# Second-layer projections as one phase of seven block products, with rows through memory and turned in each attention

## The reference, cut to what matters

```python
def dilated_mixer(h, w_in, q_norm, k_norm, positions):
    q, k, v, xq = split_cols(h @ w_in, [nh * DIL_HEAD_DIM] * 3 + [D_XA])      # nh = 12
    q = apply_rope(rms_norm(hs(q), q_norm), cos, sin)
    k = apply_rope(rms_norm(hs(k), k_norm), cos, sin)
    for g, (window, dilation) in enumerate(DIL_GROUPS):                        # (128, 1), (512, 4), (2048, 16)
        sl = slice(g * DIL_HEADS, (g + 1) * DIL_HEADS)
        o, lse = dilated_window_attention(q[:, :, sl], k[:, :, sl], v[:, :, sl], window, dilation)
    wts = jax.nn.softmax(jnp.stack(lses), axis=0)
    o = jnp.sum(wts[..., None] * jnp.stack(outs), axis=0)
```

## Time and profile before

| | us |
|---|---|
| median of three runs | 2442.65 (2440.76 to 2444.62) |
| the profiled execution | 2440.05 |
| its span in the profile | 2438.3 |
| TensorE matmul busy | 2383.5 (98%) |
| VectorE busy | 1709.8 (70%) |
| ScalarE busy | 1020.6 (42%) |
| GpSimd busy | 201.3 (8%) |

### The profile page before, as it was taken

One profiled execution on the slowest core, in us unless ns is written; L12 is line 12 of the kernel. 1 busy time (PEld: TensorE's weight loads), 2 busy tenths in 40 slices (PEclk: granted clock), 3 DMA queues, 4 the chain that ended last, 5 costly groups with the idle time before them and its releaser, 6 DMA issues. The chain is left out here.

```text
span 2438.3 us, 31873 instructions
## 1 busy us (share of the span) xinstructions
PE 2383.5 (98%) x11700; PEld 2021.3 (83%) x11700; DVE 1709.8 (70%) x2782; ACT 1020.6 (42%) x2078; POOL 201.3 (8%) x269
## 2 busy tenths in 40 slices
PE   8999999999999999999999999999999999999998
PEld 7998877888888888878788889888888888888877
DVE  4432574489999989896553462463779999998996
ACT  6433553344444444436334442333344444444443
POOL 2010021000000000002212121112100000000000
PEclk9999999999999999999999999999999999999999
DMA  4331122222222248843102111202722222227863
GB/s 154 92 92 22 37 85 67 81 80 78 84 90 87 78 136 303 272 131 139 53 18 83 36 35 48 63 30 75 219 89 83 82 78 85 88 87 258 293 190 127
DMA packets 207666, 257.69 MB, mean 106 GB/s; under 512 B 38504, under 2 KB 141912, under 8 KB 207512
## 3 DMA queue, kind: packets, MB, share of 16 engines
q1 hardware_dynamic: 203352, 255.65, 31.9%
q10 hardware_dynamic: 4160, 0.02, 0.1%
HBM read 206.54 MB, written 49.09 MB: 105 GB/s over the span
## 5 line engine op out<-in xcount | busy, mean ns | idle before, releaser
L52 PE MATMUL psum<-f_T_lo 128*128 128x512 f32 x616 | 241.6, 392 | 1.4 <-DVE f_T_lo L690 0.8
L53 PE MATMUL psum<-f_T_lo 128*128 128x512 f32 x616 | 239.8, 389 | 0.0
L54 PE MATMUL psum<-f_T_lo 128*128 128x512 f32 x616 | 239.8, 389 | 0.0
L52 PE MATMUL psum<-w_hi,hT_hi 128*128 128x512 f32 x576 | 229.3, 398 | 4.2 <-DVE w_lo L1476 2.1
L54 PE MATMUL psum<-w_hi,hT_lo 128*128 128x512 f32 x576 | 226.4, 393 | 0.0
L53 PE MATMUL psum<-w_lo,hT_hi 128*128 128x512 f32 x576 | 226.1, 393 | 0.0
L52 PEld LDWEIGHTS psum<-w_hi,hT_hi 128*128 128x128 f32 x576 | 124.8, 217 | 22.3 <-issue 3.9
L52 PEld LDWEIGHTS psum<-f_T_lo 128*128 128x128 f32 x616 | 115.6, 188 | 30.5 <-DVE f_T_lo L690 7.1
L54 PEld LDWEIGHTS psum<-w_hi,hT_lo 128*128 128x128 f32 x576 | 125.0, 217 | 18.0
L53 PEld LDWEIGHTS psum<-w_lo,hT_hi 128*128 128x128 f32 x576 | 125.1, 217 | 16.6
L52 PE MATMUL psum<-hT_hi,f_up_hi 128*128 128x512 f32 x352 | 137.4, 390 | 0.4 <-DVE f_up_lo L629 0.4
(11 more groups left out here) (432 smaller groups left out, 5919.2 us busy)
## 6 DMA issues: line engine op xcount, KB each, us to landing
raw<-in_ffn_w_up_dram SPq DMA_DIRECT2D x88, 512.0 KB, 4.7
activations<-f_act SPq DMA_DIRECT2D x44, 512.0 KB, 2.6
w_raw<-in_b_w_in_dram SPq DMA_DIRECT2D x18, 1024.0 KB, 5.7
f_up_pieces<-activations SPq DMA_DIRECT2D x30, 512.0 KB, 4.4
f_up_pieces<-in_ffn_w_down_dram SPq DMA_DIRECT2D x22, 512.0 KB, 4.8
x_between<-XY SPq DMA_DIRECT2D x16, 512.0 KB, 5.0
XY<-x_between SPq DMA_DIRECT2D x16, 512.0 KB, 6.8
w_raw<-in_a_w_in_dram SPq DMA_DIRECT2D x8, 768.0 KB, 5.6
```

The costliest lines, as they stand in the source:

```text
L52: nc.tensor.matmul(out, lhs_hi, rhs_hi, start=start, stop=False)
L53: nc.tensor.matmul(out, lhs_hi, rhs_lo, start=False, stop=False)
L54: return nc.tensor.matmul(out, lhs_lo, rhs_hi, start=False, stop=stop)
```

## The change

All projections of the second layer are done in one new phase, `rows_phase`, before the three attentions.

- The four remaining tiles of cross queries are computed first. Then six chunks follow, two for each group. A chunk has four column blocks of 384: two halves of q (or of k) of 256 columns, each beside 128 columns of v; they form a 2 x 2 block scheme with the two halves of the tokens and the two halves of the inner dimension. Each chunk is seven products of (512 tokens x 512) by (512 x 384). A product is 4 tiles x 4 parts x 3 matmuls of 384 columns.
- The token sums S1, S2, S4 are made on VectorE (high parts on ScalarE), S3 wholly on GpSimd, once. The weight differences T1 to T4 are made on VectorE for each chunk.
- The products are combined on VectorE (`put`), partly into kept tiles, partly into 16 row tiles of 128 x 384 per chunk. Row tiles stand in a ring of seven slots (`RING`). For each row tile ScalarE squares and sums two heads, GpSimd takes the root and multiplies the crossed halves by the sine, VectorE multiplies by the cosine (`turn`), GpSimd adds, ScalarE scales by the root, and SP stores the tile to memory. The gains are multiplied into the tables of sine and cosine beforehand, on GpSimd. Which tiles are squared in which product is a table, and they are scaled one product later.
- The attentions load the rows again, token tiles in the group's order, 128 x 1536 each (four blocks, each with two heads of queries or keys and one head of values). `Turns` turns queries and keys of one tile after the other in the midst of the attention's steps, in one PSUM bank: queries copied by ScalarE, keys by VectorE. In the first attention the cross queries are turned in steps 8 to 11.
- SP issues row loads at the start of the first attention (tiles 4 to 7 of its own group, the cross rows, all eight tiles of the next group), then the keys and values, then the output stores. The third group's rows are loaded during the second attention.
- `SlotsAhead` and the tile `zeros` go, and the turns in `Merge` move from steps 5 and 14 to 14 and 16.

```diff
+B11, B12, B21, B22 = range(4)
+R11, SUM2, SUM4, SUM3, R22, R12, R21 = range(7)
+BLOCK, ROPED = 384, 256
+RING = 7
+SQUARED_IN = {2: (0, 1), 3: (2, 3), 5: (4, 5, 6), 6: (7, 8, 9), 7: (10, 11, 12), 8: (13, 14, 15)}
+SCALED_IN = {p + 1: quads for p, quads in SQUARED_IN.items()}
+def rows_phase(nc, ph, psum, neg_half, hT_hi, hT_lo, ...):
...
+        W11, W21, T2, T1, T3, W22, T4 = range(7)
...
+        def wait_slot(eng, k):
+            if k >= RING:
+                eng.wait_ge(stored[k % RING], 16 * (k // RING))
...
+        @block.sync
...
+            for m in range(LASTM + 3):
+                c, j = divmod(m, 7)
+                if c < CH and j >= 3:
+                    which, last_use = {3: (B11, T1), 4: (B12, T3), 5: (B22, W22), 6: (B21, T4)}[j]
+                    sp.wait_ge(op_split, 7 * c + last_use + 1)
+                    if c + 1 < CH:
+                        load(c + 1, which)
+                    else:
+                        load_rows((B11, B12, B22, B21).index(which))
+                for c, q in due(SCALED_IN, m):
+                    store(c, q)
...
+        @block.scalar
...
+            for m in range(LASTM + 3):
+                c, j = divmod(m, 7)
+                if m == 0:
+                    enter_xq(7)
+                if c < CH and j == 1:
+                    copy_first(c)
+                if m + 1 < LASTM:
+                    high(m + 1)
...
+                for cq in due(SQUARED_IN, m):
+                    square_rows(*cq)
+                for cq in due(SCALED_IN, m):
+                    scale(*cq)
...
+        @block.vector
...
+            sum_step(sum_raw(S1), f32(A21[0]), f32(A22[0]), ALU.add, 0)
+            sum_step(sum_raw(S1), sum_raw(S1), f32(A21[1]), ALU.add, 1)
+            sum_step(sum_raw(S1), sum_raw(S1), f32(A22[1]), ALU.add, 2)
+            low(0)
+            for k in range(4):
+                norm_xq(k)
+            for m in range(LASTM + 2):
+                c, j = divmod(m, 7)
+                if c < CH and j >= 2:
+                    for which in {2: (R11,), 3: (SUM2,), 4: (SUM4,), 5: (SUM3, R22), 6: (R12,)}[j]:
+                        put(c, which)
+                if c and j == 0:
+                    put(c - 1, R21)
+                if c < CH and j == 0:
+                    make(c, T1)
+                if c < CH and j == 1:
+                    make(c, T2)
+                    make(c, T4)
+                if c < CH and j == 3:
+                    make(c, T3)
+                if m + 1 < LASTM:
+                    low(m + 1)
...
+                for cq in due(SQUARED_IN, m):
+                    turn(*cq)
...
+        @block.gpsimd
...
+            for c in range(CH):
+                for quads in SQUARED_IN.values():
+                    for q in quads:
+                        cross_rows(c, q)
+                        if q > quads[0]:
+                            add_cross(c, q - 1)
+                    n, width = root_number(c, quads[0]), 2 * len(quads)
+                    root(n, tile(c, quads[-1]) + 1, sums[:, n % 4, 0:width], rstd[:, n % 4, 0:width], P, 1.0)
+                    add_cross(c, quads[-1])
...
+        @block.tensor
...
+            for t in range(begun.TILES, TT):
+                begun.pe(pe, t, psum[:, t - begun.TILES, :], hT_hi, hT_lo).then_inc(xq_done, 1)
+            for m in range(LASTM):
+                c, j = divmod(m, 7)
+                pe.wait_ge(op_split, m + 1)
...
+                hi, lo = operands[m % 2][0:2]
+                for i in range(4):
+                    wait_bank(c, j, i)
+                    tok = slice(i * P, (i + 1) * P)
+                    for d in range(DH):
+                        last = split_matmul(nc, bank(m, i), lefts[j][0][:, d, tok], lefts[j][1][:, d, tok], hi[:, d, :], lo[:, d, :],
+                                            d == 0, d == DH - 1)
+                    last.then_inc(p_done, 1)
+class Turns:
...
+    def pe_tile(self, pe, t, keys):
+        if not keys:
+            pe.wait_ge(self.loaded[t], 16 * (self.group // 2 + 1))
+            if t == 1:
+                pe.wait_ge(self.q_out, 1)
+            elif t > 1:
+                pe.wait_ge(self.k_out, t)
+        elif t:
+            pe.wait_ge(self.q_out, t + 1)
...
+    def pe_next(self, pe, i):
+        if i < 2 * (TT - 1):
+            self.pe_tile(pe, 1 + i // 2, i % 2 == 1)
...
+    def pe_wait(self, pe, t):
+        pe.wait_ge(self.q_out, t + 1)
+        pe.wait_ge(self.k_out, t + 1)
...
         @block.tensor
         def _(pe):
+            tiles.pe_first(pe)
             for i in range(U + O_LAG):
                 if i < U:
                     heads, n = units[i][0:2]
-                    if loads and i == staged:
+                    if i < staged and i % 2 == 0:
+                        tiles.pe_wait(pe, i // 2)
+                    if i == staged:
                         pe.wait_ge(loaded, 16 * len(loads))
+                        pe.wait_ge(tiles.x_out, TT // 2)
...
         @block.sync
         def _(sp):
+            if stage.sums_due:
+                stage.store_sums(sp, stage.groups - 1)
+            row_loads(sp, -1)
             for out, src in loads:
                 sp.dma_start(out, src).then_inc(loaded, 16)
...
+                def first(sp, t):
+                    if t >= 0:
+                        return
+                    for t in range(4, TT):
+                        load_rows(sp, 0, t)
+                    turns_now[0].load_cross(sp, xq_d.rearrange("(t p) n -> p t n", p=P))
+                    for s in range(RING):
+                        sp.wait_ge(row_stored[s], 16 * len(range(s, TT + 16 * 2 * len(order), RING)))
+                    for t in range(TT):
+                        load_rows(sp, 1, t)
```

More of the change, by code:

```diff
@@ L1543, in sem @@
             return phase_semaphore(nc, ctx, f"{ph}_{name}")
-        w_hi, w_lo, base, ahead = slots.hi, slots.lo, slots.base, 2 if begun else slots.ahead
+        w_hi, w_lo, base = slots.hi, slots.lo, slots.base
         weights = [b["w"] for b in blocks]
@@ L1563, in project_phase @@
         free = {"act": sem("freed_by_act"), "dve": rows_ready}
-        ready = begun.TILES if begun else 0
-        turn_bank = [(6 + i + ready) % BANKS for i in range(2)]
+        turn_bank = [6, 7]
         def bank_of(b, t):
-            return next((3 * (G % 2) + ts.index(t) + ready) % BANKS for G, (bb, ts) in enumerate(all_groups) if bb == b and t in ts)
+            return next(3 * (G % 2) + ts.index(t) for G, (bb, ts) in enumerate(all_groups) if bb == b and t in ts)
         def wait_done(eng, T):
-            if T > ready:
-                eng.wait_ge(done, T - ready)
-        def parts_of(b):
-            return (begun.hi, begun.lo) if begun and b == 0 else (w_hi, w_lo)
+            if T:
+                eng.wait_ge(done, T)
         def groups_of(b):
@@ L1586, in _ @@
                 opening.load(sp, slots, weights[0])
-            if stage and stage.sums_due:
-                stage.store_sums(sp, stage.groups - 1)
-            for s in range(2 if opening else ahead, 2 * len(weights)):
+            for s in range(2 if opening else 0, 2 * len(weights)):
                 if s == 2:
@@ L1619, in over_tiles @@
         def over_tiles(split, tile, turn, visit):
-            for s in range(2 if opening else ahead, 2):
+            for s in range(2 if opening else 0, 2):
                 split(s)
@@ L1785, in _ @@
                                 pe.wait_ge(free[who], upto[-1])
-                    live = [t for t in group if b or t >= ready]
-                    late = begun and b == 0 and g == 1
-                    hi, lo = parts_of(b)
                     for kh in range(2):
-                        if b or not begun:
-                            pe.wait_ge(slots.split, base + 2 * b + kh + 1)
-                        for t in live:
+                        pe.wait_ge(slots.split, base + 2 * b + kh + 1)
+                        for t in group:
                             if opening and b == 0 and kh == 0:
@@ L1808, in _ @@
                             opening.norm.pe(pe, g + 2)
-                        if kh == 0 and not late:
+                        if kh == 0:
                             turns(before[:2])
-                    if late:
-                        turns(before)
                     before[:] = [(b, t) for t in group]
@@ L1828, in attention_phase @@
+def attention_phase(nc, ph, psum, ident, units, stage, turns_of, row_loads, loads=(), ahead=None, room=(), merge=None):
     U = len(units)
@@ L1921, in _ @@
                     ins.then_inc(mixed, 1)
+                tiles.pe_next(pe, i)
                 if merge:
@@ L1926, in _ @@
         def _(dve):
+            tiles.dve_keys(dve, 0)
             for i in range(U + O_LAG):
@@ L1955, in _ @@
         def _(act):
+            tiles.act_queries(act, 0)
             for i in range(U + O_LAG):
@@ L3354, in in_classes @@
[L3354 to L3363 removed]
+            rows_ctx = c.enter_context(ExitStack())
@@ L3373, in build @@
```

(10 more changed lines are left out.)

545 lines of the change are left out of this document (472 added, 73 removed).

## The result

The changed kernel takes 2506.32 us, median of 4 runs (2504.55 to 2507.83), the kernel before 2441.70 beside it: ratio 1.0264, 95% interval 1.0246 to 1.0282. Slower, as forecast, but by 65 us where I had forecast 21, and outside the range. The profiled execution took 2507.02 with a span of 2505.2, 66.9 more than before.

The account below looks back on a forecast made before the run. TensorE, busy throughout the projections, was taken as the bound. Projections 403.5 us for 442.5 and attentions 188.0 for 127.5 gave 591.5 for 570.0, +21.5 us, hence a forecast of 2463 us, range 2430 to 2486.

Parts of the forecast that it names:

- The matmuls: Projections: 2016 matmuls of 384 columns at 0.1733 us each, 349.4 us, in place of 391.7 us at 512 columns.
- the tail (+17.8): After the last product: TensorE waits 17.8 us (8 to 22) for the last row tiles to be finished and stored.
- Turning: Inside the attentions: eight added transposes a tile, handed through one bank, cost +50 us (42 to 58).
- row loads ahead of the store: First attention: 11.3 MB of loads queued before the first output store make ScalarE and TensorE wait, +9.3 us (-2.7 to 12).
- the attentions' sum: All three attentions: 127.5 us before, 188.0 us after turning, late store, clock and two phase changes fewer.
- First chunk: +12.5: First chunk of projections: TensorE waits for operands from VectorE's and GpSimd's lists, +12.5 us (0 to 18).
- Ring of seven slots: +12: Five later chunk borders: VectorE waits for tile 7's store, TensorE 2.4 us late at each; +12 us (5 to 20).
- half clock only to the attentions (+3): Before and inside the first attention: TensorE's idling brings stretches at mostly 1.2 GHz, +3 us (0 to 8).
- TensorE stays covered: Rival for the projections: first chunk, ring and most of the tail cost nothing, store not late; 2417 us, chance 0.23.
- Even: Rival: the store isn't held up (-12) and GpSimd's small operations cost half (-8); 2443 us, chance 0.12.
- The ring waits for the queue: Rival: row stores behind weight loads take 5 us, row loads hold the first attention 8 us more; 2489 us, chance 0.12.
- Clock at 1.2 GHz through the attentions: Rival: transposes don't count as work raising the clock, so attentions take up to twice as long; 2540 us, chance 0.03.

Follow-up runs that it names:

- quiet-GpSimd run: Changed kernel with S3 left out (fifth product uses S1) and 7 in 8 of the gain tables' rows left out: 2478.29 us.
- the one without S3 alone: Changed kernel with the third token sum S3 left out, the fifth product of every chunk using S1 instead: 2487.42 us.
- the third order: Changed kernel, VectorE's border list reordered: second split, two free sums, making of T1 and due turns ahead of the two sums awaiting a store: 2493.16 us.
- the first combination: Changed kernel with earlier turns, loads behind stores, S3 on VectorE (last step, split and T3 one product earlier) and the third order: 2448.62 us.
- the best kernel: The first combination with corrected lists, the last chunk's last six tiles on VectorE alone, and the first chunk's VectorE list reordered: 2431.60 us, ratio 0.9962.

## Why the prediction was wrong

**Right: the sign, and the terms beside the products.** The matmuls came at 0.1733 and the tail (+17.8) as worked out. Turning, row loads ahead of the store and tail were attacked one by one and gave 21.1, 11.5 and 5.8 us (PE's wait from 18.5 to 12.75). That the attentions' sum came out to 0.3 us is partly luck. By the forecast's terms, less 0.9 for the phase change in front of each, the first was to take 89.6 us (57.1 + 16.3 + 4.8 + 9.3 + 3 - 0.9) and took 86.9; the other two were to take 98.2 and took 100.7. The stop for the store was 9.4 us and not 12.0, and the forecast's 12.0 does not follow from its own dates either (landed at 32, wanted at 18, 2 more to resume).

**The step that failed: "First chunk: +12.5".** It cost 36.0 (26.9 of stops, 9.1 of half clock). The forecast had stops before the third, fifth and sixth product (6.7, 2.3, 3.4); the run has 5.8, 6.4, 6.1, 7.4 and 1.2 before the second to the sixth. It added up VectorE's and GpSimd's lists apart, at the durations of the earlier trace rows, without a term for what one engine does to the other's. The quiet-GpSimd run gives 8.4 us of stops with VectorE's list untouched, under the forecast's 12.5, so that list was not undersized; 18.5 us of stops came from GpSimd's work. The Trainium skill, "SBUF — State Buffer", "Who interferes with whom", says that a VectorE instruction with two SBUF inputs and a GpSimd instruction that reads SBUF hold a shared pair of ports one at a time, and that whichever issues second waits for all of the other. This trace agrees: 5.22 us for a norm of 0.88 that starts 0.07 us behind 4.62 us of GpSimd, and two of GpSimd's powers of 4 columns at 3.06 beside VectorE's sums for about 1.0 otherwise. The forecast drew no term from it.

**The term that was mis-sized: "Ring of seven slots: +12".** The mechanism and its place were right (second product of each later chunk, VectorE behind a store's landing, T1 and a split behind that). A border stops PE 3.3 to 3.9 us, not 2.4: counted from the product's start at 1318.05 the landing is at 7.4 where I had 6.3, since tile 7's scale starts at 4.7 (forecast done by 3.9) and its issue at 5.4; the landing itself was 1.9, not 2.3.

**The term that was missing: the clock in the products.** The forecast charged half clock only to the attentions (+3). The changed kernel's stops of 3.3 us or more in the products were all followed by several us at 1.2 GHz, 23 us in all, nearly as much as the whole excess forecast for this phase (24.5). The row for it was there. Over the traces of all kernels with the seven products but the one without S3 alone, stops of 3.2 to 3.9 us were followed by at least eight matmuls 0.3 us apart in 41 of 44 cases, and stops of 1.75 to 1.85 us in 2 of 12 (one in the third order, one in the first combination). So shortening a stop there mostly paid twice, but 1.8 us is not safe.

Of the rivals, *TensorE stays covered* named 2417 and the border as its point. The border can be covered, by order alone; the first chunk and the tail could only be shortened, and the best kernel stands at 2431.6. *Even* (2443) had neither of its conditions: the store was held up, and GpSimd's small operations did not cost half but more than forecast (213 us busy in the five later chunks, 43 each for 35). *The ring waits for the queue* had the time nearest to the result (2489) for a wrong reason: the store that it spoke of landed in 1.9 us. *Clock at 1.2 GHz through the attentions*: they ran at 0.91 and 0.98 in all, 1.00 from 1646 us on in the run with earlier turns; the Trainium skill's rule on transposes, which the prediction names, did not decide here.

What stays open is how much of the first chunk's remaining 18.7 us is owed to the gain tables' locks once S3 has left GpSimd. With S3 left out altogether, leaving out most of the tables' rows as well gave 9.1 us more (2487.42 to 2478.29); with S3 on VectorE it wasn't tried.

## What to carry to other kernels

Where VectorE reads two operands from SBUF while GpSimd reads it too, look for instructions of one that stretch beside the other's before adding up their lists side by side; work moved from GpSimd to the busier VectorE can then make a kernel faster. When an engine's list has a wait for a DMA's landing, look for what stands behind it and put the ready work into the wait, but delay nothing that another engine's chain needs. Price a stop of TensorE with the slow clock that may follow it. Ask of two repairs whether one only brings an engine sooner to the stop that the other removes.

## What the runs showed that was not expected

- Leaving out 20 us of GpSimd's instructions, none on VectorE's list, gave 18.9 us; leaving out most of the tables too, 28.
- Moving one split of 1.75 us out of a stall moved the stall by a product and gained nothing; two of three orders of the same instructions were 3.5 and 4.8 us slower, the third 13 us faster.
- A stop of PE of 3.3 to 3.9 us at a border of the changed kernel cost 5.6 to 6.8 us in all; ten of twelve stops of about 1.8 us left the clock at 1.00, two did not.
- Earlier turns gave 17.7 us in the attentions, loads behind the stores 7.8, and both together 33.1.
- One slot of a ring of seven was worth 15.5 us (10.4 in the profiled executions).
